# S5 preparation reordered, masks moved to ScalarE, weight transfers ahead of h, and VectorE's scan tiles laced

## What is computed

```python
for layer in range(2):
    if layer == 1: kb, vb, kmean = shared_kv(h, kv_norm, w_kv)
    h = h + 0.5 * swiglu(rmsnorm(h, ffn1_norm[layer]), ffn1_w_in[layer], ffn1_w_out[layer])
    hn = rmsnorm(h, mix_norm[layer])
    if layer < 1: h = h + s5_mixer(hn, ...)
    else:         h = h + moba_attention(hn, w_q[0], w_o[0], kb, vb, kmean)
    h = h + 0.5 * swiglu(rmsnorm(h, ffn2_norm[layer]), ffn2_w_in[layer], ffn2_w_out[layer])
return rmsnorm(h, final_norm)

# s5_mixer: 64 groups of 16 channels and 64 complex states
lam = exp(min(a_re, -1e-4) * dt) * (cos(a_im * dt) + i sin(a_im * dt))   # dt = exp(log_step)
bu  = u @ ((lam - 1) / a * b)
x_t = lam * x_{t-1} + bu_t
y   = real(x @ c) + d_skip * u
return glu(gelu(y) @ w_glu)
```

## Time and profile before

| | us |
|---|---|
| median of three runs (988.17 to 993.61) | 992.7 |
| the profiled execution, its own time | 993.64 |
| its span on the core | 991.8 |
| TensorE busy | 970.0 |
| VectorE / ScalarE / GpSimd busy | 592.4 / 492.5 / 222.3 |

### The profile page before, as it was taken

How to read it: one execution, slowest core, us unless ns; L and a number is a source line. 1 busy time by engine, 2 the same in 40 slices (tenths; PEclk the granted TensorE clock), 3 DMA queues, 4 the chain that set the end, 5 groups by cost and what they waited for, 6 DMA issues and landing times.

```text
span 991.8 us, 14595 instructions
## 1 busy us (share of the span) xinstructions
PE 970.0 (98%) x5818; PEld 803.6 (81%) x5818; DVE 592.4 (60%) x729; ACT 492.5 (50%) x708; POOL 222.3 (22%) x286
## 2 busy tenths in 40 slices
PE   7999999989899999999999999999999999999997
PEld 6888888877788888888888888888887788888886
DVE  4766755679766555555465555555566565555544
ACT  6544444346355544445453444443457554554442
POOL 4999989927200000000000000000060000000000
PEclk9999999969999999999999999999999999999999
DMA  9666666520265656665656666666661266556651
GB/s 340 219 190 188 189 178 185 169 65 4 68 188 189 186 179 189 189 202 163 212 181 191 182 190 187 182 187 190 187 184 50 88 191 188 178 189 186 191 170 42
DMA packets 48034, 169.32 MB, mean 171 GB/s; under 512 B 5984, under 2 KB 5984, under 8 KB 47968
## 3 DMA queue, kind: packets, MB, share of 16 engines
q1 hardware_dynamic: 47232, 167.80, 55.1%
q10 hardware_dynamic: 736, 0.60, 0.2%
HBM read 167.33 MB, written 1.05 MB: 170 GB/s over the span
## 4 chain that ended last, share of the span: by engine, by line
PE 74%; POOL 17%; DVE 3%; issue 3%; DMA 1%; SPq 1%; ACT 1%; POOLq 0%; DVEq 0%; ACTq 0%
PE ps L1164 70%; POOL tmp L387 7%; POOL sm L387 3%; POOL w L387 1%; PE ps L1175 1%; POOL cp L387 1%; DMA raw<-in_in 1%; POOL skip_eye L387 1%; POOL c_early L502 1%; DVE scan L1086 1%; PE ps L1188 1%; PE ps L1412 1%; POOL rotc L387 1%; POOL rots L387 0%; DVE rot_b L1093 0%
## 5 line engine op out<-in xcount | busy, mean ns | idle before, releaser
L862 DVE TENSOR_TENSOR w_lo<-raw,w_hi 128x1024 fp32r<-128x1024 f32 x311 | 395.1, 1272 | 274.0 <-ACT w_hi L607 273.3
L607 ACT ACTIVATE w_hi<-raw 128x1024 fp32r<-128x1024 f32 x311 | 328.4, 1058 | 274.9 <-PE ps L1164 272.0
L1164 PE MATMUL ps<-w_hi,x_hi 128*128 128x512 f32 x896 | 355.3, 397 | 3.8 <-DVE w_lo L862 3.8
L1164 PE MATMUL ps<-w_hi,x_lo 128*128 128x512 f32 x896 | 350.4, 391 | 0.0
L1164 PE MATMUL ps<-w_lo,x_hi 128*128 128x512 f32 x896 | 349.8, 390 | 0.0
L1164 PEld LDWEIGHTS ps<-w_hi,x_hi 128*128 128x128 f32 x896 | 169.1, 189 | 38.7 <-DVE w_lo L862 4.7
L1164 PEld LDWEIGHTS ps<-w_hi,x_lo 128*128 128x128 f32 x896 | 168.6, 188 | 36.0
L1164 PEld LDWEIGHTS ps<-w_lo,x_hi 128*128 128x128 f32 x896 | 169.0, 189 | 33.6
L1164 PE MATMUL ps<-w_hi,hid_hi 128*128 128x512 f32 x352 | 137.6, 391 | 0.0
L1164 PE MATMUL ps<-w_hi,hid_lo 128*128 128x512 f32 x352 | 137.0, 389 | 0.0
L1164 PE MATMUL ps<-w_lo,hid_hi 128*128 128x512 f32 x352 | 137.0, 389 | 0.0
(11 more groups left out here) (150 smaller groups left out, 655.4 us busy)
## 6 DMA issues: line engine op xcount, KB each, us to landing
raw<-in_in SPq DMA_DIRECT2D x175, 512.0 KB, 4.3
raw<-in_out SPq DMA_DIRECT2D x88, 512.0 KB, 3.5
raw<-in_glu SPq DMA_DIRECT2D x16, 512.0 KB, 4.2
raw<-in_k SPq DMA_DIRECT2D x8, 512.0 KB, 4.3
raw<-in_v SPq DMA_DIRECT2D x8, 512.0 KB, 4.3
raw<-in_q SPq DMA_DIRECT2D x8, 512.0 KB, 4.4
raw<-in_o SPq DMA_DIRECT2D x8, 512.0 KB, 4.3
xt<-in_xt SPq DMA_DIRECT2D x4, 256.0 KB, 5.6
```

The lines of the kernel that those rows point to most:

```text
L607: act.activation(w_hi[:, gu % WS, :], raw[:, gu % RAW, :], ACT.Copy)\
L862: dve.tensor_tensor(w_lo[:, gu % WS, :], raw[:, gu % RAW, :], w_hi[:, gu % WS, :].bitcast(F32), ALU.subtract)\
L1164: return pe.matmul(o, w, x, start=start, stop=stop, skip_group_check=True)
```

## The change

- **SyncE**: weight units 4 and 5 before tile 0 of h, unit 6 before tile 1, then 7 to 9, then b and c in one transfer each; skip rides with the gains, and a and the step come in one transfer.
- **ScalarE at the start**: the splits of units 3, 4 and 5 before the angles, the squares of h behind the split of unit 6.
- **GpSimd's preparation**: rotation tables first, then coefficients, w2, cp (signs put into two negated coefficients). VectorE's last doubling of the tables is cut into twelve halves, in block 0 of phase 1 and the first unit of block 1.
- **Masks of c** all on ScalarE, two instructions of 640 elements a tile in place of four of 320: tiles 0 to 2 in block 1 of phase 1 (`early_masks`, one a unit, waiting for cp), tiles 3 to 7 in the S5 stage. Masks of w2: two instructions of 512 elements in place of four of 256, on the engines where they were.
- **d_skip** is added by four more products on TensorE in `prepare_k` (`add_skip` is gone).
- **VectorE**: `scan_tile` is cut into five parts, and the parts of neighbouring tiles are laced; the forth rotation has buffers of its own (in `act_out` and `prod`). `low_z` goes from GpSimd to VectorE.
- **TensorE**: four products with the identity between `prepare(1)` and the second `turn_hn`; `chunk_inputs` runs two tiles ahead, `prepare_k` and `prepare` come earlier in the loop.

```diff
@@ SyncE
+            load(4)
             for q in range(TT):
+                load(5 + q)
                 sp.dma_start(h[:, q, :], io["x"][q, :, :]).then_inc(h_in[q], 16)
...
+            for gu in range(7, 10):
+                load(gu)
...
@@ ScalarE
-                        if n == 0 and b == 0 and j == 1:
+                        if n == 0 and b == 0 and j == 2:
                             s5_angles()
+                        if n == 0 and b == 0 and j == 3:
+                            input_squares()
+                        if n == 1 and b == 1 and 1 <= j <= len(early_masks):
+                            early_masks[j - 1]()
...
+            def half_c(d, g):
+                if d == 0 and g == 0:
+                    act.wait_ge(pool_step, made["cp"])
+                if d == 2 and g == 0:
+                    act.wait_ge(turns_done, 4)
+                cols = slice(S5_J * g, S5_J * g + S5_J)
+                act.activation(c_bd(d)[:, :, :, :, cols].rearrange("p r g t j -> p r (g t) j"),
...
+                               ACT.Copy, scale=half[:, g:g + 1]).then_inc(c_ready, 1)
...
             for d in range(DT):
+                if d >= 1 and d + 2 < DT:
+                    mask_c(d + 2)
                 if d + 2 < DT:
-                    prep_copy(d + 2)
-                if d + 3 < DT:
-                    mask_w(d + 3)
+                    k_copy(d + 2)
                 if d >= 1:
                     gelu(d - 1)
-                if d + 2 < DT:
-                    k_copy(d + 2)
+                if d + 3 < DT:
+                    prep_copy(d + 3)
+                if d + 4 < DT:
+                    mask_w(d + 4)
...
@@ VectorE
+            rotate_in(0)
+            combine_in(0)
+            scan_chunks(0)
             for d in range(DT):
-                if d >= 1:
-                    dve.wait_ge(st_ready, 2 * d)
-                scan_tile(d)
-            tally["x"] += DT
+                if d + 1 < DT:
+                    rotate_in(d + 1)
+                rotate_out(d)
+                if d + 1 < DT:
+                    combine_in(d + 1)
+                combine_out(d)
+                if d + 1 < DT:
+                    scan_chunks(d + 1)
+                if d >= 2:
+                    low_z(d - 2)
+            low_z(DT - 2)
...
@@ TensorE, prepare_k
+                for g in range(PPT):
+                    rows = slice(32 * g, 32 * g + 32)
+                    last = mm(ps[rows, k_bank(d), 0:32], ident[rows, rows], skip_eye[rows, d, :],
+                              False, True)
                 last.then_inc(k_done, 1)
...
@@ TensorE, the S5 stage
             prepare(1)
+            pe.wait_ge(prep_copied, 2)
+            for i in range(4):
+                mm(ps[:, prep_bank(0), 0:P], ident[:, :], ident[:, :], True, True)
             turn_hn(1)
             chunk_inputs(0)
             prepare_k(0)
             prepare_k(1)
+            chunk_inputs(1)
+            prepare(2)
             for d in range(DT):
-                if d + 1 < DT:
-                    chunk_inputs(d + 1)
                 if d + 2 < DT:
-                    prepare(d + 2)
+                    chunk_inputs(d + 2)
+                    prepare_k(d + 2)
                 direct_outputs(d)
+                if d + 3 < DT:
+                    prepare(d + 3)
...
                 state_outputs(d)
-                if d + 2 < DT:
-                    prepare_k(d + 2)
```

306 lines of the change are left out of this document (152 added, 154 removed).

## The result

| | before | after |
|---|---|---|
| median of 20 runs, us | 992.81 | 994.77 |
| lowest to highest | 987.32 to 995.66 | 993.27 to 997.15 |
| profiled execution; its span | 993.64; 991.8 | 994.25; 992.1 |
| last turn of hidden tiles of phase 0 starts | 143.31 | 145.70 |
| prepare(0) starts | 198.29 | 204.02 |

The ratio is 1.003, with a 95% interval of 1.0017 to 1.0042. So the change costs 0.2 to 0.4%, less than the bound of 0.5%. The forecast was 987.0 us with a range of 979.5 to 991.5, so it was wrong. The two traces say where: the start is 2.4 us later instead of 3.3 earlier, phase 1 behind it lasts 58.3 us instead of 55.0, and S5 with its hand-over takes 55.35 us instead of 60.10. The forecast had no step in which phase 1 gets longer, but for a late cp, and cp was in time.

The account below looks back on a forecast made before the run. TensorE was taken as three quarters of the path, GpSimd 17%; 3.3 us at the start plus 2.4 in S5 and hand-over gave 5.7, from 993.64 to 987.9, or 987.0 against the median; range 979.5 to 991.5.

Parts of the forecast that it names:

- a late cp: Rival, phase 1: cp past 175.5 us makes TensorE wait; from 184 us on slower by over 0.5%, 998 us; chance 0.05.
- Start: First units: removing TensorE's stall gives 2.3 us, the clock not dropping 1.5, a gate wait costs 0.5; 3.3 us gained.
- the gate's sum: Start: first gate's products ready by 25.8 us, TensorE wants them at 25.5, so with semaphores it waits 0.5 us.
- GpSimd's ten small steps ahead of the power: Start, lower bound: these steps come behind VectorE's and delay the first gate, leaving 0.5 us of gain.
- The bound of 0.5 us: Start's lowest gain: the gate stall grows to the size of the one removed, with a clock drop behind it again.
- the gate or an early split holds TensorE: Rival: the start gives only 0.5 us and the stage 1 to 2; 990.7 us; chance 0.06.
- GpSimd's preparation: Reordered chain before phase 1's block 1: cp ready at about 172.6 us, 2.9 to spare before 175.5; costs nothing.
- likewise: Phase 1: VectorE's twelve half-size table products fit into a unit of 2.73 us, as ScalarE's early masks do.
- Hand-over: First feed-forward half to S5: earlier power and residual; 2.0 us gained at the lower clock, 4.5 at the full clock.
- the clock does not fall in the hand-over: Rival: full clock after the last dense product; states(6) 6.9 us earlier, 8.6 with the late drop; 980.8 us; chance 0.33.
- Tiles: S5 stage: states(6) 0.7 us earlier, hand-over's 2.0 included; the clock drop at 256 us goes, 1.7 more; 2.4 together.
- The circle of ScalarE and TensorE: S5 tiles 3 to 7: prepare, copy, masks, k's products and direct_outputs depend in a ring; 6.35 us a round.

Follow-up runs that it names:

- x2_table: The changed kernel with VectorE's twelve half-size table products moved to units 3 to 8 of phase 1's block 1, two a unit; 990.84 us.
- x1_gate: The changed kernel with the squares of h ahead of the angles on ScalarE and GpSimd's power for the first gate earlier; 991.49 us.
- x3_oldstart: The changed kernel with the start's order of loads, squares and angles as before the change, and the first gate's power earlier; 992.84 us.
- x7_nomm: The changed kernel without its four products with the identity in the hand-over, the wait kept; 995.90 us.
- x9_best: The changed kernel with early squares, late angles, spread table products, c's mask before w2's, early masks behind the last split, direct_outputs(0) ahead of chunk_inputs(2); 981.33 us.

## Why the prediction was wrong, step by step

**Start: wrong in sign.** The stall and its clock loss went, as said. The step that failed is the gate's sum, "waits 0.5 us", which was 4.59. It began 2.2 us late, because the angles' request was taken from a trace in which VectorE's splits did not run beside it, and the table load of the gate (1.28) was left out. Together these are 3.5 of the 3.9 us by which the products were later than said (29.7, not 25.8); "GpSimd's ten small steps ahead of the power", which the bounds named, did come in front but ran beside the squares and cost some 0.4. TensorE reached the first gate's turn at 29.69 us, and at 29.68 before: the wait ate all that the removed stall and a first wait at 11 us, 0.9 us shorter, had given. The 2.4 us by which phase 0 ended later are the low clock behind it (4.9 us at half the speed). The bound of 0.5 us with "a drop of the clock behind it again" was the right mechanism with half the stall. The rival "the gate or an early split holds TensorE" named it and gave it 0.06 and too low a price. A reading was wrong without harm: the 1.35 us of wait for h lay before 14.44 us, not between 14.44 and 17.40.

**GpSimd's preparation: right, with luck in the number.** cp was ready at 172.70, said was 172.6, and no split waited for it. But GpSimd went on from the angles at 21.32 us instead of 19.1, so its chain was some 2 us shorter than the forecast's sum, and the two errors cancelled.

**VectorE's twelve table products: the gravest step**, one word in the text, "likewise". They were fitted into a unit at their lonely length of 0.7 us, though the earlier trace rows showed what a VectorE instruction becomes next to GpSimd (the scan, 1.77 us). At 1.5 to 1.8, beside splits of 2.0 instead of 1.2, a unit needs 3.5 us of VectorE and has 2.73: 3.3 us lost (x2_table), and any gain at the start with it (x1_gate, x3_oldstart).

**Hand-over: rival right.** The power came within 0.1 us of the mean, and the clock held: "the clock does not fall in the hand-over" (0.33) was the true case. I weighed against it that only 0.9 us of products lay there. The Trainium skill (TensorE: Matmul & The Clock Gate, Part 4: PE-mode transpose) was read as a reason for a fall; in the trace of x7_nomm, with only turns and one wait of 0.66 us for 4.1 us, the full clock stayed without a product.

**Tiles: mechanism right, size nearly.** The circle of ScalarE and TensorE set the pace, at 6.42 us, where 6.35 was said (its parts add up to 6.34, so nothing in it stood for semaphores); mask_w cost 1.33 for 1.1, mask_c 1.54 for 1.4. The drop at 256 us went. But another fall, at 215 us in a 1.17 us wait for the copy of prepare(2), was not foreseen; 6.6 us at half the speed are an estimated 3 us of work, and explain most of why the stage gained 4.75 and not the 6.9 to 8.6 of the rival. In x9_best, where direct_outputs(0) covers that wait, no fall is left.

**Sum.** Said: 3.3 + 0 + 2.4. Measured between the traces: -2.4 at the start, -3.3 in phase 1, +4.75 in the stage and 0.7 behind it (the clock at 256 us), -0.3 in all, the spans' difference.

## What to carry to other kernels

When work is moved next to a neighbour that shares a path with it, take its duration from rows where that neighbour runs, not from rows where it is alone, and add up the engine's time for a unit by those. Two losses in series can hide one another: at prepare(0) the two repairs gave 1.7 and 2.9 us alone and 7.2 together, and the old start alone gave nothing there, so a nil result of one repair does not clear its cause. Here only the traces showed it; the medians of the whole kernel added up. And a wait in an engine's queue costs what stands behind it: the same masks cost TensorE 4 us ahead of the splits, and no wait for a split behind them, although cp was later still. A trace in which a loss is gone does not show what removed it either, when the kernel without the edit is sometimes rid of it too: look at all its runs.
